# A hybrid attention encoder in fp32: the projections of z with v and of q with k as seven block products each

## The chip, the cores and the metric

The kernel runs on one core of one Trainium2 chip. TensorE (PE in the profile) multiplies, VectorE (DVE), ScalarE (ACT) and GpSimd (POOL) do the rest, and SyncE (SP) issues most of the DMAs. The metric is the device time of one launch in microseconds, lower is better. All tensors are float32.

## The reference, cut to what matters

Two layers. Each takes X (1024 tokens by 1024 channels), projects it to q, k, v (512 columns each), z (512) and x_c (256), mixes tokens in three ways, projects back, and then runs a SwiGLU block.

```python
h = rms_norm(x, norm_mix_g[l])
proj = h @ w_in[l]                       # 1024 x 2304
q, k, v, z_b, x_c = jnp.split(proj, splits, axis=-1)
mix_a = neighbourhood_attention(q, k, v, rpb)        # 8 heads
mix_b = spatial_gating(z_b, ...)         # gelu, layer norm of one half, 128x128 token matrix per head
mix_c = fourier_mix(x_c)                 # real part of a 2-D DFT over tokens and channels
mix = head_rms_norm(jnp.concatenate([mix_a, mix_b, mix_c], axis=-1), head_norm_g[l])
x = x + mix @ w_out[l]
h = rms_norm(x, norm_ffn_g[l])
x = x + (jax.nn.silu(h @ w_gate[l]) * (h @ w_up[l])) @ w_down[l]
```

## The kernel before, in words

**fp32 products out of three.** A float32 operand is split into a high part (rounded to the type fp32r, which TensorE reads at full rate) and the rest, the low part. `split3` (L1870 to L1874) issues three matmuls per tile into one PSUM bank: high by high, low by high and high by low. So each weight piece (128 by 1024, two k-tiles of 512 columns, 512 KB) is loaded by SP into a slot (`w_raw`), gets its high part on ACT (`piece_hi`, `w_hi`, L761) and its low part on POOL (`piece_lo`, `w_lo`, L675). POOL's instruction is what raises `w_ready`, for which PE waits before it uses a piece (`wait_piece`).

**Order of the work.** Nothing is scheduled at run time. Each engine has one list of instructions, written by hand, and they meet at semaphores. In a layer X lies transposed in SBUF, channels on the partitions: `x_res` raw, `h_hi` and `h_lo` times the norm's gain but not yet divided by the root mean square. PE makes x_c first (8 k-steps, 256 columns), then z, then a position DFT, then v, the spatial matrices and a channel DFT, then q, then k, then attention. A projection (`project`) fills all eight banks over eight k-tiles, 192 matmuls of 512 columns. The factor 1/rms is one number per token (`rstd_tok`, made on POOL by a power) and is put in when the banks are evicted: by ACT for z (with the gelu, L896), by ACT and DVE for v, by DVE for q and k (L1383, L1413, with the factor spread over the partitions by way of DRAM). Every result is a complete sum in its bank, evicted once. SP loads the pieces of the next projection while PE works on the last, and ACT's list has the `w_hi` of a projection's first pieces ahead of, or among, the evictions of the one before it.

**Around it.** DVE makes the Fourier butterflies (L1296 to L1309), the layer norm of z, the head norms of mix_b and mix_c (a reduction, a power of 32 columns on POOL at L695, a broadcast product at L1368), and in attention the logits (L1404). X stays in SBUF through attention and receives the out-projection and the SwiGLU result.

## Time and profile before

| | us |
|---|---|
| median of three runs | 2064.92 (2064.7 to 2065.62) |
| span of the profiled execution | 2062.8 |
| PE busy | 2042.2, 99% |
| DVE busy | 1419.9, 69% |
| ACT busy | 825.1, 40% |
| POOL busy | 227.8, 11% |

The span is from the first to the last instruction of one profiled execution; no time of its own is given for that execution beside it, and the runs lie 1.9 to 2.8 us above it. Start and length of an instruction in a timeline row are in microseconds from the span's start. TensorE's matmuls are pipelined, so a matmul of 0.39 us that starts 0.23 us after the one before it costs 0.23 us. An engine's busy share says little without the list it works through: what matters here is whether something that PE waits for is late. The profile has PE idle for 8.5 us at the start and for about 6 us in all after it.

### The profile page before, as it was taken

To read this page: it belongs to the slowest core of one execution; us is meant where nothing else is said; L and a number is where in the kernel's file an instruction comes from. 1 tells how busy PE (TensorE), PEld (TensorE's weight loads), DVE (VectorE), ACT (ScalarE), POOL (GpSimd) and SP (SyncE) were. 2 spreads that over 40 slices of the span, in tenths; PEclk is the share of its full clock that TensorE was granted. 3 is DMA by queue.
4 is the path that set the end of the run, shared out by engine and by line. 5 is a ranking of instruction groups with operands and counts; after the bars stand their busy time and mean duration, and the time that the engine had idled before them with its cause. 6 is when DMAs were issued, how large, how long until landed. Compare 5 with 4: busy or idle time off the path is not lost.

```text
span 2062.8 us, 27797 instructions
## 1 busy us (share of the span) xinstructions
PE 2042.2 (99%) x10316; PEld 1698.2 (82%) x10316; DVE 1419.9 (69%) x2320; ACT 825.1 (40%) x1466; POOL 227.8 (11%) x135
## 2 busy tenths in 40 slices
PE   8999999999999999999999999999999999999998
PEld 7888788888888888888898887888888888888887
DVE  6323773789877778787833338647988777778877
ACT  4221683452333333444612227634433333344443
POOL 1332034200000000000023301441000000000000
PEclk9999999999999999999999999999999999999999
DMA  5222443224333236633221314441243323383333
GB/s 183 72 92 62 144 134 123 72 77 169 130 111 107 98 112 255 195 97 97 76 86 62 102 41 144 144 153 48 85 172 129 114 93 111 109 310 114 97 98 123
DMA packets 111060, 244.40 MB, mean 118 GB/s; under 512 B 13648, under 2 KB 18640, under 8 KB 110672
## 3 DMA queue, kind: packets, MB, share of 16 engines
q1 hardware_dynamic: 97056, 214.32, 32.4%
q10 hardware_dynamic: 13872, 28.31, 3.7%
q8 instruction: 83, 1.36, 0.3%
q14 instruction: 49, 0.40, 0.1%
HBM read 191.73 MB, written 50.86 MB: 118 GB/s over the span
## 4 chain that ended last, share of the span: by engine, by line
PE 92%; DVE 5%; issue 1%; ACT 1%; DMA 0%; ACTq 0%; POOL 0%; DVEq 0%
PE bank L1872 28%; PE bank L1874 28%; PE bank L1873 28%; PE bank L2036 2%; PE bank L2055 2%; PE bank L2020 2%; DVE s_lo L1233 1%; DVE t_lo L1536 0%; PE bank L1966 0%; PE bank L2077 0%; PE bank L1995 0%; PE bank L2070 0%; ACT logits L950 0%; DVE hid_cu L1649 0%; ACT s_hi L797 0%
## 5 line engine op out<-in xcount | busy, mean ns | idle before, releaser
L1872 PE MATMUL bank<-t_hi,s_hi 128*128 128x512 f32 (+1 forms) x1336 | 516.9, 387 | 0.8 <-DVE hid_cu L1649 0.5
L1873 PE MATMUL bank<-t_lo,s_hi 128*128 128x512 f32 (+1 forms) x1336 | 516.3, 386 | 0.0
L1874 PE MATMUL bank<-t_hi,s_lo 128*128 128x512 f32 (+1 forms) x1336 | 516.3, 386 | 0.0
L1872 PEld LDWEIGHTS bank<-t_hi,s_hi 128*128 128x128 f32 x1336 | 250.9, 188 | 52.6 <-DVE hid_cu L1649 1.4
L1874 PEld LDWEIGHTS bank<-t_hi,s_lo 128*128 128x128 f32 x1336 | 250.9, 188 | 50.9
L1873 PEld LDWEIGHTS bank<-t_lo,s_hi 128*128 128x128 f32 x1336 | 250.9, 188 | 50.6
L675 POOL TENSOR_TENSOR w_lo<-w_raw,w_hi 128x1024 fp32r<-128x1024 f32 x65 | 161.1, 2492 | 928.9 <-ACT w_hi L761 787.4
L1872 PE MATMUL bank<-b_hi,s_hi 128*128 128x512 f32 x528 | 206.0, 390 | 0.2
L1874 PE MATMUL bank<-b_hi,s_lo 128*128 128x512 f32 x528 | 205.5, 389 | 0.0
L1873 PE MATMUL bank<-b_lo,s_hi 128*128 128x512 f32 x528 | 205.4, 389 | 0.0
L1872 PE MATMUL bank<-h_hi,w_hi 128*128 128x512 f32 x512 | 201.1, 393 | 0.0
L1874 PE MATMUL bank<-h_hi,w_lo 128*128 128x512 f32 x512 | 199.5, 390 | 0.0
L1873 PE MATMUL bank<-h_lo,w_hi 128*128 128x512 f32 x512 | 199.3, 389 | 0.0
L797 ACT ACTIVATE s_hi<-w_u 128x512 fp32r<-128x512 f32 x142 | 89.6, 631 | 233.0 <-PE bank L1874 176.3
L797 ACT ACTIVATE s_hi<-w_down 128x512 fp32r<-128x512 f32 x154 | 97.3, 632 | 200.7 <-PE bank L1874 199.9
L1233 DVE TENSOR_TENSOR s_lo<-w_down,s_hi 128x512 fp32r<-128x512 f32 x154 | 107.6, 699 | 75.8 <-ACT s_hi L797 75.7
L797 ACT ACTIVATE s_hi<-w_g 128x512 fp32r<-128x512 f32 x142 | 89.4, 630 | 163.9 <-PE bank L1874 104.9
L1872 PE MATMUL bank<-w_hi,h_hi 128*128 128x512 f32 (+1 forms) x384 | 137.4, 358 | 8.6 <-DVE h_lo L1128 8.5
L1873 PE MATMUL bank<-w_lo,h_hi 128*128 128x512 f32 (+1 forms) x384 | 136.6, 356 | 0.0
L1874 PE MATMUL bank<-w_hi,h_lo 128*128 128x512 f32 (+1 forms) x384 | 136.6, 356 | 0.0
L761 ACT ACTIVATE w_hi<-w_raw 128x1024 fp32r<-128x1024 f32 x67 | 70.3, 1058 | 127.5 <-DMA w_raw<-in_win 109.4
L1872 PEld LDWEIGHTS bank<-b_hi,s_hi 128*128 128x128 f32 x528 | 99.1, 188 | 21.3 <-issue 0.9
(218 smaller groups left out, 3187.2 us busy)
## 6 DMA issues: line engine op xcount, KB each, us to landing
w_g<-in_wg SPq DMA_DIRECT2D x44, 512.0 KB, 3.5
w_u<-in_wu SPq DMA_DIRECT2D x44, 512.0 KB, 4.4
t_raw<-hidden_t SPq DMA_DIRECT2D x88, 256.0 KB, 2.6
bias<-in_bias SPq DMA_DIRECT2D x24, 768.0 KB, 5.8
w_raw<-in_win SPq DMA_DIRECT2D x34, 512.0 KB, 3.8
t_raw<-hidden_b SPq DMA_DIRECT2D x66, 256.0 KB, 2.6
hidden_b<-hid_g SPq DMA_DIRECT2D x60, 256.0 KB, 2.0
hidden_t<-hid_x SPq DMA_DIRECT2D x44, 256.0 KB, 2.0
```

The lines of the kernel that those rows point to most:

```text
L675: nc.gpsimd.tensor_tensor(WL[s][:, :], WR[s][:, :], WH[s][:, :], ALU.subtract).then_inc(w_ready, 1)
L761: nc.scalar.activation(WH[s][:, :], WR[s][:, :], ACT.Copy).then_inc(w_hi, 1)
L797: nc.scalar.activation(SH[q % W_RING][:, :], weight_block(q), ACT.Copy).then_inc(s_hi, 1)
L1233: nc.vector.tensor_tensor(SL[q % W_RING][:, :], weight_block(q), SH[q % W_RING][:, :], ALU.subtract)\
L1872: nc.tensor.matmul(bank, lh, rh, start=start, stop=False)
L1873: nc.tensor.matmul(bank, lh, rl, start=False, stop=False)
L1874: return nc.tensor.matmul(bank, ll, rh, start=False, stop=stop)
L2020: mm = nc.tensor.matmul(score_bank(i, e).rearrange("p (r c) -> p r c", c=KC), qs[hp, c, q0:q0 + P], grid(ks[hp, c, :])[:, 4 * rr:4 * rr + ...
L2036: mm = nc.tensor.transpose(B[2 + t % 2][:, n * P:(n + 1) * P], L[:, t % 4, n * P:(n + 1) * P], IDENT[:, :])
L2055: mm = nc.tensor.matmul(B[VALUE_BANK][e * DH:(e + 1) * DH, c * P:(c + 1) * P], VB[j % 2][:, rr + n, h * DH:(h + 1) * DH], PT[:, h % 4, n * ...
```

## The change

q with k, and z with v, form two pairs. For each pair, X is cut into four blocks (token half by channel half: b11, b12, b21, b22), the two weight matrices into four (channel half by which of the two), and the two results, each in token halves, come out of seven block products instead of eight, in the Winograd form of Strassen's scheme. A block product is 16 tiles (4 banks by 4 k-tiles) of three matmuls. The 14 products are interleaved in the order of `IN_PRODUCTS`; the document numbers them n0 to n13 by their place in it. One group uses banks 4 to 7 (zv), the other banks 0 to 3 (qk). The banks are not cleared between most products: the sums run on in PSUM, and after each product its four banks are read out ("tapped") into a result, ACT writing and DVE adding.

Since blocks of different tokens are now added, X must be normalised before the products. 1/rms is turned and spread over the partitions by PE (`spread_tokens`), DVE multiplies X in place (`norm`, 16 instructions of 128x512), makes the block differences in place (`differences`, 16), and ACT and DVE split seven operands into high and low parts (`operand`, `operand_low`, 28 instructions each). Weight blocks are summed by POOL (`block_sum`, `third_sum`, 20 instructions of 128x1024 a layer), a sum that is used twice goes through DRAM (`w_sum_zv`, `w_sum_qk`), and 28 pieces a layer are split instead of 16. Raw X, now overwritten, is kept in DRAM (`x_scratch`; for layer 0 the input itself) and read back during attention.

```diff
+IN_PRODUCTS = (("zv", 2), ("qk", 2), ("qk", 1), ("zv", 1), ("zv", 6), ("qk", 6), ("qk", 7), ("zv", 7),
+               ("zv", 4), ("qk", 4), ("zv", 5), ("qk", 5), ("zv", 3), ("qk", 3))
+IN_TERMS = {2: ((1, 0),), 1: ((0, 0),), 6: ((0, 1), (0, 0), (1, 1)), 7: ((0, 1), (0, 0)), 4: ((1, 1),),
+            5: ((0, 1), (1, 1)), 3: ("s2", (1, 0))}
+ACT_TAPS = [n for n in range(NPROD) if IN_PRODUCTS[n][1] in (2, 6, 7) or IN_PRODUCTS[n] == ("qk", 4)]
...
 # GpSimd
+            def block_sum(l, n):
+
+                for i in range(2):
+                    s = ALL_SLOT[piece(n, i)]
+                    pool.wait_ge(w_landed[s], 16 * (l * PER_SLOT[s] + loads_before(piece(n, i)) + 2))
+                    nc.gpsimd.tensor_tensor(WR[s][:, :], WR[s][:, :], WT[s][:, :], ALU.add).then_inc(w_sum, 1)
+            def blocks_lo(l, *products):
+                for n in products:
+                    for i in range(2):
+                        if n in IN_THIRDS:
+                            pool.wait_ge(s2_stored, 16 * w_thirded(l, n, 1))
+                        piece_lo(l, piece(n, i))
...
+                blocks_lo(l, 4)
+                block_sum(l, 5)
+                third_sum(l, 5)
+                blocks_lo(l, 5)
+                pool.wait_ge(hs_var, l * 2 + 1)
+                nc.gpsimd.tensor_tensor(SR[:, :], SS[:, :], NHALF[:, :], ALU.pow).then_inc(hs_rstd, 1)
+                block_sum(l, 6)
+                blocks_lo(l, 6)
+                block_sum(l, 7)
+                blocks_lo(l, 7, 8, 9)
...
+                block_sum(l, 13)
                 pool.wait_ge(ln_var, l + 1)
                 nc.gpsimd.tensor_tensor(LR[:, :], LR[:, :], NHALF[:, 0:8], ALU.pow).then_inc(ln_rstd, 1)
...
 # ScalarE
+            def blocks_hi(l, *products):
+                for n in products:
+                    for i in range(2):
+                        piece_hi(l, piece(n, i))
+                def tap(n, *banks):
+
+                    g, product = IN_PRODUCTS[n]
+                    for j in banks or range(4):
+                        act.wait_ge(acc_full, full(l, n, j))
...
+                tap(4)
+                operand("t3")
+                blocks_hi(l, 5)
+                tap(5)
+                blocks_hi(l, 6)
+                tap(6)
+                operand("t4")
+                blocks_hi(l, 7)
+                tap(7)
+                operand("m1")
+                blocks_hi(l, 8)
+                tap(8)
+                blocks_hi(l, 9)
+                operand("b22")
+                tap(9)
+                blocks_hi(l, 10)
...
 # VectorE
+                def norm(k, h):
...
+                    nc.vector.scalar_tensor_tensor(out=X[:, k, half(h)], in0=X[:, k, half(h)], scalar=GM[:, k:k + 1],
+                                                   in1=(B[6] if h else RL)[:, :], op0=ALU.mult, op1=ALU.mult)\
+                        .then_inc(x_normed, 1)
+                for k in range(4):
+                    norm(4 + k, 1)
+                    if k:
+                        operand_low("b21", k - 1)
+                operand_low("b21", 3)
+                for k in range(4):
+                    norm(k, 1)
+                copy_xc(6, 7)
+                variance(0)
+                for k in range(4):
+                    operand_low("b11", k)
+                copy_xc(2, 3)
...
 # TensorE
+                    if j == 0 and k % 2 == 0:
+                        wait_piece(piece(n, k // 2))
...
+                for k in range(4):
+                    for j in range(2):
+                        in_ready(0, j, k)
+                        in_tile(0, j, k)
+                    if k == 1:
+                        sum_tokens(0)
+                spread_tokens(0)
+                in_bank(0, 2)
+                in_bank(0, 3)
+                in_product(1)
+                pe.wait_ge(fft_step, (l + 1) * FFT_STEPS)
...
+                position_dft(0, (4, 5, 6))
+                position_dft(1, (7, 4, 5))
+                in_bank(2, 0)
+                in_bank(2, 1)
...
+                pe.wait_ge(ab_act, l * 3 + 3)
+                pe.wait_ge(ab_dve, l * 3 + 3)
+                channel_dft(0)
+                channel_dft(1)
+                in_bank(2, 2)
+                in_bank(2, 3)
+                for n in range(3, NPROD - 1):
+                    in_product(n)
+                in_bank(NPROD - 1, 0)
+                pe.wait_ge(ln_step, l * 10 + 10)
+                spatial(0)
...
 # SyncE
+                for k in range(0, KT_D, 2):
+                    sp.dma_start(X[:, k:k + 2, :], (xscr if l else x)[k:k + 2].rearrange("k p n -> p k n"))\
+                      .then_inc(x_moved, 16)
```

**ScalarE in the middle of the projections.** Before, with `w_hi` the high parts of weight pieces (the number is the buffer) and `uv_tok` the evicted z:

```order
L761 ACTIVATE w_hi_80<-w_raw_104 128x1024 [waits w_landed2]
L761 ACTIVATE w_hi_78<-w_raw_102 128x1024 [waits w_landed0]
L761 ACTIVATE w_hi_79<-w_raw_103 128x1024 [waits w_landed1]
L896 ACT_TABLE_LOAD
L896 ACTIVATE uv_tok<-bank,rstd_tok 128x2x256 [waits acc_full] x8
```

The conversions wait for their landing alone and stand ahead of the evictions of z. In the changed kernel, from the taps of n4 (`v_tok`) over those of n5 (`q_raw`) to those of n6 (`k_raw`), where `w_hi_94` and `w_hi_95` are n5's weights, `104` and `105` those of n6, `96` and `97` those of n7:

```order
L1057 ACTIVATE v_tok<-bank 128x512 [waits acc_full] x4
L927 ACTIVATE in_t_hi<-x_res 128x512 [waits t_raw,acc_full] x4
L903 ACTIVATE w_hi_94<-w_raw_124 128x1024 [waits w_third]
L903 ACTIVATE w_hi_95<-w_raw_125 128x1024 [waits w_third]
L1060 ACTIVATE q_raw<-bank 128x8x4x16 [waits acc_full] x4
L903 ACTIVATE w_hi_104<-w_raw_134 128x1024 [waits w_sum]
L903 ACTIVATE w_hi_105<-w_raw_135 128x1024 [waits w_sum]
L1062 ACTIVATE k_raw<-bank 128x512 [waits acc_full] x4
L927 ACTIVATE in_t_hi<-x_res 128x512 [waits t_raw,acc_full] x4
L903 ACTIVATE w_hi_96<-w_raw_126 128x1024 [waits w_sum]
L903 ACTIVATE w_hi_97<-w_raw_127 128x1024 [waits w_sum]
```

The high parts of a product's weights now stand behind the four taps of the product before it.

**GpSimd in the same place.** Before, the low parts of v's and q's pieces around the layer norm's power:

```order
L675 TENSOR_TENSOR w_lo_90<-w_raw_102,w_hi_78 128x1024 [waits w_hi]
L690 TENSOR_TENSOR ln_rstd<-ln_rstd,minus_half 128x8 [waits ln_var]
L675 TENSOR_TENSOR w_lo_98<-w_raw_110,w_hi_86 128x1024 [waits w_hi]
L675 TENSOR_TENSOR w_lo_99<-w_raw_111,w_hi_87 128x1024 [waits w_hi]
L675 TENSOR_TENSOR w_lo_91<-w_raw_103,w_hi_79 128x1024 [waits w_hi]
```

In the changed kernel, from n4's low parts to n6's sums (L786 adds the second block, L793 the third):

```order
L774 TENSOR_TENSOR w_lo_111<-w_raw_126,w_hi_96 128x1024 [waits w_hi,s2_stored]
L774 TENSOR_TENSOR w_lo_112<-w_raw_127,w_hi_97 128x1024 [waits w_hi,s2_stored]
L786 TENSOR_TENSOR w_raw_124<-w_raw_124,w_term_139 128x1024 [waits w_landed0]
L786 TENSOR_TENSOR w_raw_125<-w_raw_125,w_term_140 128x1024 [waits w_landed1]
L793 TENSOR_TENSOR w_raw_124<-w_raw_124,w_term_139 128x1024 [waits w_landed0]
L793 TENSOR_TENSOR w_raw_125<-w_raw_125,w_term_140 128x1024 [waits w_landed1]
L774 TENSOR_TENSOR w_lo_109<-w_raw_124,w_hi_94 128x1024 [waits w_hi,s2_stored]
L774 TENSOR_TENSOR w_lo_110<-w_raw_125,w_hi_95 128x1024 [waits w_hi,s2_stored]
L820 TENSOR_TENSOR head_rstd<-head_ss,minus_half 128x32 [waits hs_var]
L786 TENSOR_TENSOR w_raw_134<-w_raw_134,w_term_149 128x1024 [waits w_landed10]
L786 TENSOR_TENSOR w_raw_135<-w_raw_135,w_term_150 128x1024 [waits w_landed11]
```

Between n4's low parts and n5's stand four sums, and n6's sums stand behind n5's low parts and a power.

**VectorE between the butterflies and the DFT's copies.** Before, from the last butterfly's successor to the copies of the DFT's banks (`dft_t`, which the channel DFT reads):

```order
L1309 SCALAR_TENSOR_TENSOR dft_69<-dft_sums,dft_even_odd 128x256 x4
L1317 BN_STATS bn_stats<-uv_tok 128x6 [waits z_ev]
L1320 BN_AGGR mean_var<-bn_stats 128x2 [waits ln_stat]
...
L1322 TENSOR_SCALAR ln_rstd<-mean_var 128x8 [waits ln_stat]
L1327 COPY dft_t<-bank 128x512 [waits dft_full] x2
L1327 COPY dft_t<-bank 128x256 [waits dft_full]
```

In the changed kernel, where `rstd_low` is 1/rms of the first token half, in SBUF, and `in_n` the operand of n4 and n5:

```order
L1579 SCALAR_TENSOR_TENSOR dft_86<-dft_sums,dft_even_odd 128x256 x4
L1487 SCALAR_TENSOR_TENSOR x_res<-x_res,g_mix,rstd_low 128x512 [waits x_squared,xc_act] x8
L1503 TENSOR_TENSOR x_res<-x_res 128x512 [waits x_normed]
L1506 SCALAR_TENSOR_TENSOR in_n_85<-x_res 128x512 [waits t_raw,acc_full]
L1509 SCALAR_TENSOR_TENSOR x_res<-in_n_85,x_res 128x512 [waits t_raw]
L1511 SCALAR_TENSOR_TENSOR x_res<-in_n_85,x_res 128x512
L1592 COPY dft_t_70<-bank 128x512 [waits dft_full] x2
L1592 COPY dft_t_70<-bank 128x256 [waits dft_full]
```

Eight normalisations and four differences, all from SBUF to SBUF, have moved ahead of the copies.

## Rows read from the trace of the kernel before

**Rows 1.** The page: span, and the engines' busy time
```profile
span 2062.8 us, 27797 instructions
PE 2042.2 (99%) x10316; PEld 1698.2 (82%) x10316; DVE 1419.9 (69%) x2320; ACT 825.1 (40%) x1466; POOL 227.8 (11%) x135
```

**Rows 2.** Timeline, TensorE: start, length, engine, line; four places
```profile
35.05 0.47 PE L1872 MATMUL bank<-w_hi,h_hi 128*128 128x512 f32 x1
...
73.65 0.39 PE L1872 MATMUL bank<-w_hi,h_hi 128*128 128x512 f32 x1
...
78.41 0.39 PE L1872 MATMUL bank<-w_hi,h_hi 128*128 128x512 f32 x1
...
223.26 0.45 PE L2020 MATMUL bank<-k_hi,q_hi 64*128 64x384 f32 x2
...
369.56 1.05 PE L1866 MATMUL bank<-ident,rstd_tok_ffn 128*128 128x128 f32 x8
```

**Rows 3.** Busy time of each engine in the stretch of z, v, q and k
```profile
core 0: us, PE busy (x) PEld busy (x) DVE busy (x) ACT busy (x) POOL busy (x), PEclk, DMA share, GB/s
35.00:223.30 188.30, 188.20 (x846) 155.00 (x845) 67.49 (x91) 43.59 (x61) 48.01 (x18) 1.00 0.21 65
```

**Rows 4.** Timeline, TensorE at the start
```profile
8.87 0.41 PE L1873 MATMUL bank<-w_lo,h_hi 128*128 128x256 f32 x1
...
12.47 0.28 PE L1872 MATMUL bank<-w_hi,h_hi 128*128 128x256 f32 x1
12.59 0.28 PE L1873 MATMUL bank<-w_lo,h_hi 128*128 128x256 f32 x1
```

**Rows 5.** Groups of instructions by line: busy us, mean ns, idle before
```profile
L675 POOL TENSOR_TENSOR w_lo<-w_raw,w_hi 128x1024 fp32r<-128x1024 f32 x65 | 161.1, 2492 | 928.9 <-ACT w_hi L761 787.4 <-DVE t_lo L1243 111.6 <-DVE w_lo L1249 29.7
L761 ACT ACTIVATE w_hi<-w_raw 128x1024 fp32r<-128x1024 f32 x67 | 70.3, 1058 | 127.5 <-DMA w_raw<-in_win 109.4 <-DMA w_raw<-in_wom 16.0 <-DMA w_raw<-in_wout 2.1
L695 POOL TENSOR_TENSOR head_rstd<-head_ss,minus_half 128x32 f32<-128x32 f32 x4 | 21.7, 5429 | 12.4 <-DVE head_ss L1363 12.4
L959 ACT ACTIVATE k_hi<-k_raw 128x512 fp32r<-128x512 f32 x16 | 10.1, 632 | 63.2 <-DVE k_raw L1413 63.2
L1391 DVE TENSOR_TENSOR k_lo<-k_raw,k_hi 128x512 fp32r<-128x512 f32 x16 | 11.1, 693 | 11.2 <-ACT k_hi L959 11.2
L1413 DVE SCALAR_TENSOR_TENSOR k_raw<-bank,rstd_mix 128x512 f32<-128x512 f32 x16 | 11.1, 692 | 53.1 <-PE bank L1874 53.1
L680 POOL TENSOR_TENSOR rstd_tok_ffn<-rstd_tok_ffn,minus_half 128x4 f32<-128x4 f32 x5 | 5.0, 1006 | 648.8 <-DVE rstd_tok_ffn L1152 614.6 <-DVE rstd_tok_ffn L1523 34.2
```

**Rows 6.** Timeline, VectorE, Fourier sums of layer 0
```profile
38.98 1.23 DVE L1296 TENSOR_TENSOR dft_even_odd<-xc_tok 128x1024 f32<-128x1024 f32 x1
40.12 3.42 DVE L1297 TENSOR_TENSOR dft_even_odd<-xc_tok 128x1024 f32<-128x1024 f32 x1
...
46.33 1.43 DVE L1309 SCALAR_TENSOR_TENSOR dft<-dft_sums,dft_even_odd 128x256 f32<-128x256 f32 x4
```

**Rows 7.** Timeline of layer 1: VectorE, then GpSimd
```profile
1060.30 2.77 DVE L1299 TENSOR_TENSOR dft_sums<-dft_even_odd 128x512 f32<-128x512 f32 x1
...
1056.38 6.14 POOL L675 TENSOR_TENSOR w_lo<-w_raw,w_hi 128x1024 fp32r<-128x1024 f32 x2 [2.68 <-ACT w_hi L761]
```

**Rows 8.** Timeline, VectorE and GpSimd in the attention's tail
```profile
312.20 0.68 DVE L1455 COPY att_heads<-bank 128x512 f32<-128x512 f32 x1
...
311.52 4.75 POOL L675 TENSOR_TENSOR w_lo<-w_raw,w_hi 128x1024 fp32r<-128x1024 f32 x2
```

**Rows 9.** DMA issues: count, KB each, us to landing
```profile
w_raw<-in_win SPq DMA_DIRECT2D x34, 512.0 KB, 3.8
```

**Rows 10.** Timeline, VectorE, first scores of layer 0
```profile
224.29 0.56 DVE L1404 CUSTOM_DVE_ANT_0 logits<-bank,bias 128x384 f32<-128x384 f32 x1 [0.20 <-PE bank L2020]
227.67 0.55 DVE L1404 CUSTOM_DVE_ANT_0 logits<-bank,bias 128x384 f32<-128x384 f32 x1
```

**Rows 11.** Busy time and DMA in a stretch of attention
```profile
255.00:270.00 15.00, 15.00 (x163) 12.42 (x161) 11.75 (x35) 13.17 (x37) 4.53 (x5) 1.00 0.04 9
```

More of the change, by code:

```diff
@@ L80, with loads_before @@
+LOADS = [1, 1] + [len(IN_TERMS[product]) for _, product in IN_PRODUCTS for _ in range(2)] + [1] * 16
+SLOTS = 15
+USED_ORDER = list(range(OUT_P, OUT_P + 7))
+PER_SLOT = [sum(n for t, n in zip(ALL_SLOT, LOADS) if s == t) for s in range(SLOTS)]
+def loads_before(p):
+    return sum(n for t, n in zip(ALL_SLOT[:p], LOADS) if t == ALL_SLOT[p])
 BANKS = [4, 5, 6, 7, 0, 1, 2, 3]
@@ L84 @@
 FFT_STEPS = 13
[L86 to L88 removed]
+X_ORDER = [(k, 1) for k in range(KT_D)] + [(k, 0) for k in range(KT_D)]
 PRODUCTS = (1, 2, 5, 6, 3, 7, 4)
@@ L123, in x_final, with summed @@
     return (20, 28)[k >= 4] + k % 4 + 1 if h else (36, 40)[k >= 4] + k % 4 + 1
-def summed(order, i):
-    h = order[i][1]
-    second = [j for j, (_, hh) in enumerate(order) if hh == h][1]
-    last = max(i, second)
-    return sum(order[j] != next(o for o in order if o[1] == order[j][1]) for j in range(last + 1))
+def summed(i):
+    return i - (i > 8)
 KB = 1024
@@ new lines, in load_block, with load_blocks, store_sum @@
+            def load_block(l, n, t):
+                for i in range(2):
+                    load_piece_of(l, n, t, i)
+            def load_blocks(l, n, behind=None):
+                if behind is not None:
+                    sp.wait_ge(acc_full, full(l, behind, 3))
+                for t in range(min(len(IN_TERMS[IN_PRODUCTS[n][1]]), 2)):
+                    load_block(l, n, t)
+            def store_sum(l, n):
+                for i in range(2):
+                    sp.wait_ge(w_third, w_thirded(l, n, i))
+                    sp.dma_start(sscr[IN_PRODUCTS[n][0]][i], WR[ALL_SLOT[piece(n, i)]][:, :]).then_inc(s2_stored, 16)
@@ L457, in load_out, with store_values @@
+            def store_values(n, first):
+                for j in range(4):
+                    b = first + j
+                    wait_tapped(sp, l, n, j)
+                    sp.dma_start(vscr[b * P:(b + 1) * P, :], VN[:, b, :]).then_inc(v_stored, 16)
             def load_out(l, p):
@@ new lines, in operand @@
+                def operand(name):
+                    for k in range(4):
+                        in_operand_hi(l, name, k)
+                blocks_hi(l, 0)
+                for i in range(12, 16):
+                    x_hi(l, *X_ORDER[i])
+                    x_square(l, i)
+                operand("b21")
+                copy_xc(4, 5)
+                blocks_hi(l, 1)
+                operand("b11")
+                copy_xc(0, 1)
+                act.wait_ge(r_spread, 2 * l + 2)
+                nc.scalar.activation(RL[:, :], B[1][:, :], ACT.Copy).then_inc(xc_act, 1)
@@ new lines, in _ @@
+                operand("t3")
[13 more added lines that the diff above has]
+                blocks_hi(l, 10)
+                act.wait_ge(acc_full, full(l, 9, 3))
+                for c in range(4):
+                    act.wait_ge(tap_act, l * 4 * len(ACT_TAPS) + 4 * ACT_TAPS.index(9) + c + 1)
+                    nc.scalar.activation(KH_[:, c, half(1)], KR_[:, c, half(1)], ACT.Copy).then_inc(qk_hi, 1)
@@ new lines, in _ @@
+                differences(0)
+                for b in range(3):
+                    dve.wait_ge(dft_full, l * 8 + 3 + b + 1)
+                    a = slice(2 * b, min(2 * b + 2, 5))
+                    nc.vector.tensor_copy(AB[1][:, a, :],
+                                          B[(7, 4, 5)[b]][:, 0:256 * (a.stop - a.start)]
+                                          .rearrange("p (a n) -> p a n", n=256)).then_inc(ab_dve, 1)
+                for k in range(1, 4):
+                    tap(2, k - 1)
+                    differences(k)
+                    operand_low("n2", k - 1)
@@ L1471, in _ @@
                     else:
-                        key_rest(7)
+                        for c in range(4):
+                            query_rest(0, c)
                     if i == 5:
@@ L1960, in position_dft, with in_bank, in_product @@
+                def in_bank(n, j):
+                    for k in range(4):
+                        in_ready(n, j, k)
+                        if n == NPROD - 1 and j == 3 and k == 2:
+                            scores(0)
+                        in_tile(n, j, k)
+                def in_product(n):
+                    for j in range(4):
+                        in_bank(n, j)
                 def position_dft(f, banks):
```

908 lines of the change are left out of this document (517 added, 391 removed).

## The prediction, made before the changed kernel ran

> **What bounds the kernel now.** I read the page first: PE busy 2042 of 2063 us [rows 1]. Only PE's time counts, and any wait of PE beyond today's handful is a loss. The timeline of PE then gives its price: 21 matmuls of 128x512 from 73.65 to 78.41, 0.2267 us each [rows 2]. In layer 0 z starts at 35.05 and the first scores stand at 223.26 [rows 2]; in this stretch PE is busy for 188.20 of 188.30 us, with DVE at 67, ACT at 44, POOL at 48 us and the DMA at 0.21 [rows 3]. So the projections run at PE's full rate, and the others only have to be on time. The question is therefore what each engine's list makes PE wait for afterwards, and I went through the five lists for that, with durations from the groups by line [rows 5].
>
> **What it removes.** A layer has 768 matmuls of 512 columns for z, v, q and k; 14 products of 48 are 672. 96 x 0.2267 = 21.8 us a layer saved, 43.5 in all. One product is 10.9 us. This is certain, since it is a count of PE work.
>
> **What it adds on PE.** Two spreads a layer, of four transposes (eight instructions) each, 0.8 us apiece (369.56 to the next matmul at 370.37 [rows 2]): 1.6.
>
> **What it adds on POOL.** 28 low parts and 20 sums in place of 16 low parts. A low part costs 2.4 (two take 4.75 [rows 8]; the mean of 2.49 holds some stretched ones [rows 5]). The trace has no POOL sum of f32; it has the same two inputs and size as a subtraction, so 2.4; from below it could be no less than half (two powers of 32 columns take 5.4 each and 4 columns 1.0 [rows 5], so its price is not by bytes alone), from above 3.1 (two low parts stretched to 6.14 beside DVE [rows 7]). 48 x 2.4 = 115 us a layer, within the 188 of the stretch, but in bursts.
>
> **DVE beside POOL.** On DVE an addition from SBUF to SBUF starts at 40.12 and takes 3.42, while its twin takes 1.23 [rows 6]; another takes 2.77 where a low part runs on POOL [rows 7]. A copy from PSUM beside POOL keeps its 0.68 [rows 8]. I conclude that a two-input operation within SBUF waits until the running POOL operation ends. In the new list 16 norms, 16 differences and 28 operand low parts are of this kind. Alone one is 0.69 (`k_lo` [rows 5]); in a string against back-to-back POOL operations each costs a whole one, 2.4 + 0.6 = 3.0. Bounds: 0.69 (nothing blocks) and 3.42 [rows 6].
>
> **The chain between products.** This is what decides. PE finishes bank 3 of product n; ACT taps it (0.63, as `k_hi` of that size [rows 5]), and only then, by its list, makes the high part of n+1's first piece (1.06), POOL its low part (2.4), and only then may PE start n+1. With 0.2 of drain and 0.2 of semaphores that is 4.5 us of idle PE before n6, n9 and n10. Before n5, n7 and n8 ACT also has four operand conversions, 4 x 0.63 = 2.5, in the way: 7.0. In the old list the conversions stand ahead of the evictions, which is why PE never waits there [rows 3]. The second piece's low part comes 2.4 after the first, which feeds only 6 matmuls, 1.36: + 1.04 each time. Special cases: before n5 POOL has two sums, two thirds whose third term is loaded after the second (512 KB in 3.8 [rows 9]), and a store: 7.5 instead of 7.0; before n6 it has the power of 32 columns (5.4 [rows 5]) and two sums, and DVE's head scaling beside it: 5.3. Together 8.5 + 6.4 + 8.0 + 8.0 + 5.5 + 5.5 = 41.9 us a layer. n11 and n12 have their weights in time, since ACT makes them apart from the last taps.
>
> **Ahead of n5.** The first spread waits for the power of 4 columns (1.0 [rows 5]) behind two low parts on POOL: 3.0 in layer 0, 0 in layer 1, where they are made earlier. The other spread waits until DVE has done norms, x_c copies, variance and four low parts, some blocked: 6.5 (7.2 in layer 1). Then DVE does its butterflies, 6.6 us without the blocked piece (38.98 to 47.76, less 2.2 [rows 6]), and eight norms and four differences opposite eight POOL operations that run back to back, before it copies the DFT's banks: PE waits 2.4 before the position DFT and 2.8 before the channel DFT, 5.2 in all.
>
> **The end.** The layer norm's power now stands on POOL behind the sums of n13, and n13's low parts behind that. PE waits 4.0 for its first piece, 3.3 for the second, and 4.2 before the spatial matrices for the two passes over 2048 columns, `q_lo` and `k_lo` that stand between on DVE: 11.5. In attention the third logits come 3.4 after the first today (224.29 and 227.67 [rows 10]); afterwards between them stand the power (5.4), head scaling of 2048 columns (2 x 1.14, the pitch of 1024 in [rows 6]) and four `q_lo` (2.6), with 1.0 for the scaling before the power: 11.3, so + 7.9.
>
> **Hidden.** X's return is 4 MB, in a stretch where DMA is at 0.04 [rows 11] and nothing needs it before the out-projection: nothing; uncovered it would be some 30 us (8 x 3.8 [rows 9]). The stores and further loads: DMA at 0.21 [rows 3], nothing; if one is late, see the rivals. 16 taps on DVE from PSUM replace evictions of the same kind (0.69, L1413 [rows 5]).
>
> **PE's clock after a wait.** From 8.87 to 12.47, after PE's first idle 8.5 us, 17 matmuls of 256 columns start at a pitch of 0.21; from 12.47 to 12.59 it is 0.12 [rows 4]. That is the lower level (1.2 GHz) and then the upper (2.4). A restart after a long wait thus costs 17 x (0.21 − 0.12) ≈ 1.6 to 1.8 us. The trace has such a restart only after 8.5 us of idling, none after 2 to 5 us. I charge it to the waits of 6.5 and more and to nothing shorter: the one before the second spread (1.8) and those before n5, n7 and n8, where the slow matmuls fall partly into the wait for the second piece (0.8 each): 4.2 a layer, 8.4 in all. Bounds: 0 and a charge for each wait, 13.8 a layer.
>
> The Trainium skill ("TensorE: Matmul & The Clock Gate", section "Part 1: The HAM clock gate") says that an array that idles falls back to 1.2 GHz and that sustained work gives 2.4 back; it sets no charge per wait that I could take over. The trace agrees at its one place, the first 3.6 us of work at half pitch [rows 4]. If each of the new waits counted as such, my sum would go to the upper bound, which is the first rival.
>
> **The sum.** Layer 0: 3.0 + 1.6 + 6.5 + 5.2 + 41.9 + 11.5 + 7.9 = 77.6, less 21.8 = + 55.8. Layer 1: 0 + 1.6 + 7.2 + 5.2 + 41.9 + 11.5 + 7.9 = 75.3, less 21.8 = + 53.5. With 8.4 for the clock, + 117.7. On the profiled execution 2062.8 [rows 1] becomes 2180.5; the median lies 2.1 above its span and becomes 2064.9 + 117.7 = 2182.6.
>
> **Rivals.**
> Every wait, the short ones too, restarts PE at the lower level: 13.8 a layer in place of 4.2. For it, the start [rows 4]; against it, no short wait in the trace shows it either way. 2064.9 + 109.3 + 27.6 = 2202.
>
> DVE and POOL hardly hinder each other in a string, and only the chain between products stays (40.5, some of n5's and n6's extra gone), with 5.2 at the DFTs, 1.6, 5 at the end and 6 in attention: 58.3 − 21.8 = 36.5 a layer, 2138. For it, only two of the traced DVE operations that I name are blocked; against it, the butterfly that is blocked to 3.42 [rows 6].
>
> Loads come late: a block's second and third terms take another 4 to 5 us each beside one another (8.3 instead of 3.8), about 9 a layer at n5 and the sums after it: 2200. Against it, DMA at 0.21 [rows 3].
>
> The other side: PE never waits between products, because ACT and POOL convert n+1's weights while PE works on n. The saving then stands, less the spreads: 2064.9 − 43.5 + 3.2 = 2024.6. It decides from the point where `w_hi` of n+1 is made before the last tap of n. The old list does it [rows 3], and there are over 6 us of ACT and POOL time free per product; the new list puts the taps first for six products of fourteen, so it can't hold for those. Even if all else were free, 6 x 4.5 a layer of chain is 54, more than the 43.5 saved. That the change isn't what it says is not to be seen: the count is 672.
>
> **How the numbers follow.** The forecast has 0.72, the clock at every wait 0.13, little hindrance 0.10, late loads 0.03, the other side 0.02. The unknown prices: the POOL sum at 3.1 instead of 2.4 adds some 10 us over 20 sums a layer of which a third are in PE's way; the strings on DVE at 0.69 take off up to 20; the clock's bounds are −8 and +19. So the forecast alone goes from 2150 to 2212, and the range with parts of its rivals from 2125 to 2222. Less than 0.2% can't be told from no change; faster by more 0.02, within 0.01, slower 0.97.
>
> **What would show it.** PE's list of idle times: before n5, n7, n8 about 7 to 8.5 us, before n6, n9, n10 about 4.5 to 5.5, each ended by POOL's low part, and one of about 1 us six matmuls later; none before n11 and n12. First scores of layer 0 at about 271 (275 with the clock) instead of 223.3. POOL busy for about 115 us of each projection stage. Norms on DVE at about 3 us beside POOL. Matmuls at a pitch of 0.4 for some 3 us behind the longest waits only. Wrong it would be if the waits between products are ended by something else or are missing, or if the pitch of whole products is off 0.2267.

## The result, and the profile after

The changed kernel takes 2196.49 us (2195.94 to 2199.15), the kernel before 2065.14: slower by 6.4% (ratio 1.0638, 95% interval 1.0623 to 1.0654). 2182 was forecast, in a range of 2125 to 2222. Of 131 us lost 118 were foreseen. Of all the runs below one was slow (one of four of dft_act, 7211 us at a granted clock of 0.39), and its ratio is made without it.

The page of the changed kernel, first lines (beside [rows 1]):

```profile
span 2194.1 us, 28110 instructions
## 1 busy us (share of the span) xinstructions
PE 2053.7 (94%) x10156; PEld 1694.8 (77%) x10156; DVE 1548.5 (71%) x2463; ACT 903.6 (41%) x1611; POOL 405.8 (18%) x202
```

The span grew by 131.3. PE has 160 instructions fewer (192 matmuls less, 32 of the spreads more) and is yet busy for longer, 2053.7 against 2042.2. So the loss has two forms: PE idles, and PE is busy at a slower clock. The waits of PE over the whole run (engine, line, who released it: us, times, longest):

```profile
PE bank L2158 <- POOL w_lo L774: 75.2, 17, 8.7
PE bank L2309 <- DVE minus_max L1693: 15.9, 2, 8.0
PE bank L2272 <- ACT dft_t L1090: 10.9, 2, 5.7
PE bank L2191 <- DVE xc_tok L1475: 10.7, 2, 5.8
PE bank L2158 <- DVE h_lo L1331: 9.6, 1, 9.6
PE bank L2288 <- DVE v_tok L1527: 7.6, 2, 3.8
```

Of these only the wait for `h_lo`, at the start, was there before. 75 us are waits for the low part of a weight piece, made by POOL. What such a wait is made of is seen between n6 and n7 of layer 0, in the timeline (start, length, engine, line; the bracket is the idle time before and who ended it):

```profile
162.47 0.39 PE L2160 MATMUL bank<-in_t_hi,w_lo 128*128 128x512 f32 x1
162.90 0.60 ACT L1062 ACTIVATE k_raw<-bank 128x512 f32<-128x512 f32 x1 [2.12 <-PE bank L2160]
163.39 2.18 ACT L927 ACTIVATE in_t_hi<-x_res 128x512 fp32r<-128x512 f32 x4
165.47 1.99 ACT L903 ACTIVATE w_hi<-w_raw 128x1024 fp32r<-128x1024 f32 x2
166.59 4.67 POOL L774 TENSOR_TENSOR w_lo<-w_raw,w_hi 128x1024 fp32r<-128x1024 f32 x2 [10.33 <-ACT w_hi L903]
168.99 0.79 PE L2158 MATMUL bank<-w_hi,in_t_hi 128*128 128x512 f32 x1 [6.12 <-POOL w_lo L774]
```

The tap, four operand conversions, the high part, the low part: each step begins only when the one before it is done or nearly so, since ACT's list has them in this order. POOL had idled for 10.33 us before. The matmuls that follow, and two from far behind a wait:

```profile
169.58 0.63 PE L2159 MATMUL bank<-w_lo,in_t_hi 128*128 128x512 f32 x1
170.00 0.63 PE L2160 MATMUL bank<-w_hi,x_lo 128*128 128x512 f32 x1
...
233.56 0.39 PE L2159 MATMUL bank<-w_lo,in_m_hi 128*128 128x512 f32 x1
233.79 0.39 PE L2160 MATMUL bank<-w_hi,x_lo 128*128 128x512 f32 x1
```

Other starts of layer 0 that waited for POOL, before n5, n6, n9, and both pieces of n13:

```profile
131.20 0.80 PE L2158 MATMUL bank<-in_n_hi,w_hi 128*128 128x512 f32 x1 [8.54 <-POOL w_lo L774]
149.30 0.80 PE L2158 MATMUL bank<-in_t_hi,w_hi 128*128 128x512 f32 x1 [4.05 <-POOL w_lo L774]
205.66 0.80 PE L2158 MATMUL bank<-in_t_hi,w_hi 128*128 128x512 f32 x1 [4.06 <-POOL w_lo L774]
260.24 0.80 PE L2158 MATMUL bank<-in_b_hi,w_hi 128*128 128x512 f32 x1 [2.95 <-POOL w_lo L774]
264.60 0.50 PE L2158 MATMUL bank<-in_b_hi,w_hi 128*128 128x512 f32 x1 [1.43 <-POOL w_lo L774]
```

From 169.58 the matmuls start 0.43 apart; at 233.56, far from a wait, 0.23, as before [rows 2]. That is 1.2 and 2.4 GHz; the granted clock is 0.50 from 169.6 to 174.0 and 1.00 from 233.5 to 236.0. Layer 0 from 35 to 300 us had 90 starts at the slow pitch, which cost 20.1 us, layer 1 has 74, 17.1 us (pitch less 0.2267, summed over the rows). A few of these starts are of the spatial product, whose pitch is 0.43 at the full clock too, and two of its matmuls at the lower clock, 0.85 apart, are left out; with both put right the cost is 20.8 and 17.2.

The first scores of layer 0 stand at 282.2, those of layer 1 at 1364.3 (before: 223.26 [rows 2] and 1242.2). With 8.0 us more of waiting just behind them, layer 0 lost 66.9 us and layer 1 63.2, 130.1 of the 131.3.

### The profile page after: what moved, and what is told of

Its sections match the earlier page's. It is cut to its first block, busy times and chain, and to the rows that moved or that the text cites. A ratio compares the mean times of both kernels' runs of the same rounds, so it can differ in the third digit from the quotient of the medians.

```text
span 2194.1 us, 28110 instructions
## 1 busy us (share of the span) xinstructions
PE 2053.7 (94%) x10156; PEld 1694.8 (77%) x10156; DVE 1548.5 (71%) x2463; ACT 903.6 (41%) x1611; POOL 405.8 (18%) x202
## 4 chain that ended last, share of the span: by engine, by line
PE 80%; DVE 7%; POOL 6%; issue 3%; ACT 3%; DMA 1%; ACTq 0%; DVEq 0%; SPq 0%; POOLq 0%
PE bank L2158 24%; PE bank L2159 24%; PE bank L2160 24%; POOL w_lo L774 4%; PE bank L2360 2%; PE bank L2379 2%; POOL w_raw L786 2%; PE bank L2309 2%; ACT w_hi L903 1%; DMA w_raw<-in_win 1%; DVE q_lo L1645 1%; DVE s_lo L1433 1%; POOL head_rstd L836 0%; DVE x_sq_sum_first L1346 0%; PE bank L2288 0%
## 5 line engine op out<-in xcount | busy, mean ns | idle before, releaser
L774 POOL TENSOR_TENSOR w_lo<-w_raw,w_hi 128x1024 fp32r<-128x1024 f32 x90 | 234.7, 2626 | 927.8 <-ACT w_hi L903 804.3
L779 POOL TENSOR_TENSOR rstd_tok_ffn<-rstd_tok_ffn,minus_half 128x4 f32<-128x4 f32 x5 | 5.0, 1006 | 648.6 <-DVE rstd_tok_ffn L1352 614.5
L903 ACT ACTIVATE w_hi<-w_raw 128x1024 fp32r<-128x1024 f32 x91 | 93.0, 1050 | 63.2 <-DMA w_raw<-in_win 30.5
L2160 PEld LDWEIGHTS bank<-b_hi,s_lo 128*128 128x128 f32 x528 | 99.1, 188 | 20.7
L2159 PEld LDWEIGHTS bank<-b_lo,s_hi 128*128 128x128 f32 x528 | 99.1, 188 | 20.3
L1443 DVE TENSOR_TENSOR t_lo<-t_raw,t_hi 128x512 fp32r<-128x512 f32 x154 | 105.5, 685 | 8.7 <-ACT t_hi L969 8.7
L1433 DVE TENSOR_TENSOR s_lo<-w_g,s_hi 128x512 fp32r<-128x512 f32 x142 | 97.4, 686 | 10.7 <-ACT s_hi L963 10.7
L2158 PE MATMUL bank<-h_hi,w_hi 128*128 128x512 f32 x256 | 101.1, 395 | 0.0
```

The source lines that it names most:

```text
L774: nc.gpsimd.tensor_tensor(WL[s][:, :], WR[s][:, :], WH[s][:, :], ALU.subtract).then_inc(w_ready, 1)
L903: nc.scalar.activation(WH[s][:, :], WR[s][:, :], ACT.Copy).then_inc(w_hi, 1)
L1433: nc.vector.tensor_tensor(SL[q % W_RING][:, :], weight_block(q), SH[q % W_RING][:, :], ALU.subtract)\
L1443: nc.vector.tensor_tensor(TL[t][:, :], TR[t][:, :], TH[t][:, :], ALU.subtract).then_inc(t_lo, 1)
L2158: nc.tensor.matmul(bank, lh, rh, start=start, stop=False, skip_group_check=reopened)
L2159: nc.tensor.matmul(bank, lh, rl, start=False, stop=False, skip_group_check=reopened)
```

## The experiments

Times are medians; "changed kernel" is 2196.49 us, and all ratios are to the kernel before, which ran beside each of them at 2065.05 to 2065.86.

**hi_first: the conversions of n+1 inside the taps of n.** For n = 4 to 9, on ScalarE:

```diff
-                tap(6)
-                operand("t4")
-                blocks_hi(l, 7)
+                tap(6, 0)
+                blocks_hi(l, 7)
+                tap(6, 1, 2, 3)
+                operand("t4")
```

> ScalarE converts the two weight pieces of n+1 behind the first tap of n instead of behind the fourth (n = 4 to 9). Theory (the order of ScalarE's list makes the waits between the products): the waits before n7 to n10 (6.3, 6.3, 4.2, 4.2 us a layer) go, and with them some 7.7 us of matmuls at half pitch; n6 keeps about 3 of 4.2 (power and sums on GpSimd stand before it) and n5 its 8.7 (the store of its sum). 30 us a layer: 2196.5 - 60 = about 2137 us. Rival (GpSimd has too much to do, and the order only shows it): the waits come back in front of n7 to n10 as waits for GpSimd, and half or less is gained, 2165 or more.

2144.25 us, ratio 1.0380 (1.0365 to 1.0396): 52 gained of 60 expected. Its waits of PE:

```profile
PE bank L2164 <- POOL w_lo L774: 40.5, 12, 10.1
PE bank L2315 <- DVE minus_max L1699: 15.9, 2, 8.0
PE bank L2278 <- ACT dft_t L1090: 10.9, 2, 6.2
```

The waits before n7 to n10 are gone in both layers; n6 keeps 3.2 and 4.3, n5 8.7 and 10.3. The 8 us that are missing of the 60 stand at n13, whose wait grew from 3.1 to 5.0, in n5 of layer 1, in n6, and in the slow pitch, which fell by 12 us where 15 were expected. The order of one list made the waits before n7 to n10, and POOL had room for the same work earlier.

**small_sums: GpSimd's sums cut, the order kept.** Both sums of weight blocks:

```diff
-nc.gpsimd.tensor_tensor(WR[s][:, :], WR[s][:, :], WT[s][:, :], ALU.add)
+nc.gpsimd.tensor_tensor(WR[s][:, 0:8], WR[s][:, 0:8], WT[s][:, 0:8], ALU.add)
```

> The 20 sums of weight blocks a layer add 8 columns instead of 1024 (the rest of each sum is left out), so GpSimd has some 50 us a layer less to do, with every wait and the order as it was. Theory (order, not load): the waits before n6 to n10 stay, n5 loses 2 to 3 us and n13 some, stretched VectorE operations shorten: about 2185 us. Rival (GpSimd's load and its contention with VectorE make the loss): 2150 us or less.

2177.08 us, ratio 1.0538 (1.0521 to 1.0556): 19 gained. The waits before n6 to n10 are 4.2, 6.3, 6.3, 4.2, 4.2 us with the sums and without them. So the load of POOL isn't their cause. The 19 come from n5 (8.7 to 6.4), the DFT (5.4 to 3.0) and n13.

**fill: PE kept busy in the waits.** TensorE, ahead of the weights' waits of n5 to n10:

```diff
+FILL = {5: 34, 6: 16, 7: 25, 8: 25, 9: 16, 10: 16}
...
+                        for i in range(FILL[n]):
+                            nc.tensor.matmul(B[bank][:, :], t[:, 0, 0:P], t[:, i % 4, :], start=False,
+                                             stop=i == FILL[n] - 1, skip_group_check=True)
```

> TensorE does 16 to 34 matmuls of 512 columns with operands it has while it would wait for the weights of n5 to n10 (they add to a bank, so the result is changed). Theory (the lower clock after each of these waits comes from the idling): the matmuls at half pitch behind n5 to n10 go (13.2 us a layer), the wait for the second piece comes back to 1.04 six times, so 7 us a layer less, about 2182 us. Rival (the half pitch has another cause, such as late weights): 2196 us with the same half pitch. If only waits over 6.5 us had the charge, as my forecast assumed, the gain would be 2 to 3 us a layer.

2187.39 us, ratio 1.0591 (1.0575 to 1.0606): 9 gained where 14 were expected. The mechanism is plain all the same. Windows over n5 to n12 of layer 0, first of the changed kernel, then of this one (us; busy time of PE, PEld, DVE, ACT, POOL; PEclk, DMA share, GB/s):

```profile
122.00:256.00 134.00, 101.04 (x382) 79.76 (x382) 45.51 (x55) 46.09 (x70) 78.93 (x31) 0.86 0.33 119
```

```profile
122.00:252.00 130.00, 120.92 (x519) 96.22 (x518) 45.46 (x54) 45.91 (x69) 80.04 (x31) 1.00 0.35 126
```

The granted clock goes from 0.86 to 1.00; of 58 starts at the slow pitch (13.0 us) none is left. Nothing but filler was added, so idling caused them, after the waits of 4.1 us too. The weights are no earlier, so what PE gains in clock it partly waits for again: with fast matmuls the second piece is late by 0.8 us at n5 to n8 and by 1.3 at n9 and n10, which matmuls at the lower clock had hidden.

**dft_act and dft_dve: what holds the position DFT.** In the changed kernel PE waits 5.2 us there. The timeline of SyncE's queue, ScalarE and PE:

```profile
69.84 3.14 SPq L527 DMA_DIRECT2D w_term<-in_win  x2
...
70.65 1.05 ACT L903 ACTIVATE w_hi<-w_raw 128x1024 fp32r<-128x1024 f32 x1
...
73.02 2.05 SPq L527 DMA_DIRECT2D w_raw<-in_win  x3
...
78.48 1.06 ACT L903 ACTIVATE w_hi<-w_raw 128x1024 fp32r<-128x1024 f32 x1 [6.79 <-DMA w_raw<-in_win]
79.45 1.34 ACT L1090 ACTIVATE dft_t<-bank 128x512 f32<-128x512 f32 x3
...
80.08 1.22 PE L2272 MATMUL bank<-twiddle,dft 128*128 128x256 f32 x2 [5.21 <-ACT dft_t L1090]
```

ScalarE waits for n3's second piece, which SyncE issues only behind n4's third terms (69.84; its own issue is among those at 73.02), and the DFT's copies stand behind it. dft_act moves that one conversion behind the copies:

```diff
-                blocks_hi(l, 3)
+                piece_hi(l, piece(3, 0))
...
                         .then_inc(ab_act, 1)
+                piece_hi(l, piece(3, 1))
```

> The changed kernel with one edit: ScalarE converts the second weight piece of n3 behind its copies of the DFT's banks, not ahead of them. Theory (the wait of 5.4 and 5.8 us before the second position DFT comes from a load that SyncE issues late and behind which ScalarE's copies stand): this wait falls to about 1, with some half pitch, 2196.5 - 8 to 12 = 2184 to 2188 us. Rival (my forecast's cause, VectorE's norms and differences stretched beside GpSimd's sums): no change, 2196.

dft_dve moves what my forecast had named:

```diff
-                differences(0)
                 for b in range(3):
...
                                           .rearrange("p (a n) -> p a n", n=256)).then_inc(ab_dve, 1)
+                differences(0)
```

> The changed kernel with one edit: the first four differences on VectorE stand behind its copies of the DFT's banks. My forecast's cause (these stretched operations hold the copies) gives 5 us or more, under 2190. The theory from the trace (a late load holds ScalarE) gives nothing: 2196.

dft_act: 2182.87 us, ratio 1.0569 (1.0554 to 1.0585), 13.6 gained, and the wait is gone in both layers. dft_dve: 2194.06 us, ratio 1.0628 (1.0614 to 1.0642), 2.4 gained, which the intervals don't tell from nothing. The late load held PE. VectorE's differences had a small part in it all the same, by another way than the forecast's: in dft_dve the wait falls from 5.4 and 5.8 us to 3.5 and 4.5, and the DFT begins 1.5 us sooner behind the second spread in both layers. SyncE may load the third terms only when GpSimd's first sums of n4 are made, and beside the differences these take longer. The two sums in the changed kernel, then in dft_dve:

```profile
66.97 5.62 POOL L786 TENSOR_TENSOR w_raw<-w_raw,w_term 128x1024 f32<-128x1024 f32 x2
...
67.04 4.73 POOL L786 TENSOR_TENSOR w_raw<-w_raw,w_term 128x1024 f32<-128x1024 f32 x2
```

This is also why small_sums shortened the wait to 3.0.

**att: the head scaling later.** VectorE:

```diff
                 tap(13, 3)
-                head_scale(1, MB)
...
+                    if i == 2:
+                        head_scale(1, MB)
```

> The changed kernel with one edit: mix_b's head scaling on VectorE, which waits for GpSimd's power of 5.4 us, stands behind the sixth logits of the layer instead of ahead of the third. Forecast's step (the power and the scaling cost 7.7 of the 8.0 us wait in attention, four low parts the rest): the wait of 8.0 falls to about 2.8, 2196.5 - 2 x 5.2 = about 2186 us. Rival (the wait is moved, since the tiles of mix_b are turned soon after): 2192 or more.

2187.87 us, ratio 1.0592: 8.6 gained of 10.4. The wait at the second scores falls from 8.0 to 2.8 in both layers.

**all_moved: all of it at once.** hi_first, dft_act, and on GpSimd each power ahead of the pieces it stood behind (the head norm's behind n6's), n5's sums ahead of n4's low parts, n13's high parts earlier on ScalarE, head scaling after six logits:

```diff
-                blocks_lo(l, 4)
                 block_sum(l, 5)
                 third_sum(l, 5)
+                blocks_lo(l, 4)
...
-                block_sum(l, 13)
                 pool.wait_ge(ln_var, l + 1)
                 nc.gpsimd.tensor_tensor(LR[:, :], LR[:, :], NHALF[:, 0:8], ALU.pow).then_inc(ln_rstd, 1)
+                block_sum(l, 13)
```

> The same work in another order: ScalarE converts n+1's pieces behind the first tap of n, n13's ahead of k's last high parts, and n3's second piece behind the DFT copies; GpSimd makes n5's sums ahead of n4's low parts, each power of rstd, head and layer norm ahead of (or, for the head norm, behind) the weights it stood beside; VectorE scales mix_b's heads after six logits. Theory (the loss is all order): waits fall from 63 to under 10 us a layer and the half pitch with them, 2064.9 - 43.5 + 3.2 + 10 to 20 = 2035 to 2045 us, faster than the kernel before. Rival (the pipeline's own latencies of landing, sum, high and low part don't fit between two products): 2065 to 2090.

2105.04 us, ratio 1.0191 (1.0176 to 1.0206). 91 of 131 us are back, but neither theory is right: no product waits long for its pipeline (n7 2.8 us, n12 0.8), and still 30 us of waits a layer remain. Its waits:

```profile
PE bank L2296 <- DVE v_tok L1534: 22.0, 2, 11.0
PE bank L2280 <- ACT dft_t L1090: 14.0, 2, 7.2
...
PE bank L2166 <- POOL w_lo L774: 7.5, 6, 2.6
PE bank L2199 <- DVE xc_tok L1482: 6.1, 2, 3.5
```

The two large ones end in VectorE. Its timeline in all_moved, and in the middle what GpSimd does then:

```profile
67.00 11.64 DVE L1494 SCALAR_TENSOR_TENSOR x_res<-x_res,g_mix,rstd_low 128x512 f32<-128x512 f32 x8
...
69.91 5.54 POOL L793 TENSOR_TENSOR w_raw<-w_raw,w_term 128x1024 f32<-128x1024 f32 x2
...
78.68 1.36 ACT L1090 ACTIVATE dft_t<-bank 128x512 f32<-128x512 f32 x3 [11.25 <-DVE x_res L1494]
...
182.78 11.09 DVE L1646 TENSOR_TENSOR k_lo<-k_raw,k_hi 128x512 fp32r<-128x512 f32 x4
206.41 11.00 DVE L1662 TENSOR_SCALAR uv_tok<-uv_tok,mean_var,ln_rstd 128x256 f32<-128x256 f32 x8 [6.15 <-POOL ln_rstd L832]
```

In the changed kernel the same eight norms took 5.38 us with POOL idle beside them. Here four `k_lo` take 11.09 beside back-to-back sums and low parts, 2.8 each for 0.69 of work [rows 5]. Once the order no longer leaves POOL idle, VectorE is what it pushes aside.

**dft_pool: GpSimd holds back.** all_moved, and:

```diff
                 blocks_lo(l, 2)
+                pool.wait_ge(x_normed, l * 16 + 16)
                 block_sum(l, 4)
```

with n3's second piece loaded ahead of n4's third terms.

> The kernel all_moved, and GpSimd starts the sums of n4 only when VectorE has normalised X's second half; SyncE loads n3's second piece ahead of n4's third terms. Theory (an operation of GpSimd keeps VectorE's two-input operations within SBUF out, so that less GpSimd work at that time makes TensorE faster): the wait of 7.3 and 7.0 us at the second position DFT falls under 2 and its half pitch with it, 2105 - 12 to 15 = 2090 to 2093 us. Rival (GpSimd's sums are then late and n4 or n5 waits instead): 2100 or more.

2101.83 us, ratio 1.0177 (1.0162 to 1.0191): 3 us less than all_moved, which is the rival's case. The wait of 7.3 at the DFT is gone, and one of 6.1 stands before n4, ended by VectorE's `v_tok`. What was won at one place was paid at the next.

**all2, all3, all4: VectorE's strings cleared.** all2 brings the layer norm's power and its passes earlier (n12's sum ahead of n10's low parts), spreads k's low parts between taps, and makes and uses the first rstd sooner. all3 moves copies, one tap and the head norm's reduction. all4 takes eight differences off n4's path, for which the operand has memory of its own:

```diff
-        N2 = at("in_n2", IN_LO_AT["n2"], [P, 4, HALF])
+        N2 = at("in_n2", IN_LO_AT["b21"], [P, 4, HALF])
...
                 operand_low("n2", 3)
+                tap(3, 1, 2)
+                for k in range(4):
+                    differences_rest(k)
```

> dft_pool, and: the sum of n12 ahead of n10's low parts, the layer norm's power ahead of n12's low parts and its passes with less GpSimd work beside them, k's low parts between the taps of n10 or behind the last taps, the head power behind n7's low parts, the rstd of the first half made and used earlier, q's last low parts between the first logits. Theory: of the waits left in all_moved (11.2 at the spatial matrices, 2.8 at n7, 3.7 at the spread, 2.8 in attention) most go, with their half pitch: 2090 - 2 x 18 = about 2055 us, faster than the kernel before by about 0.5%. Rival (GpSimd has 126 us of work a layer in 190 and VectorE can't be kept clear of it): the waits only move, 2075 to 2090.

> all2, and six moves more: VectorE copies the DFT's banks ahead of the first four differences; ScalarE makes n4's high parts before the last two of the operand n2; the first tap of n3 stands before the last differences; the head norm of mix_b is reduced behind the first two logits and scaled after the sixth; v's rows are loaded ahead of the second bias tile. Theory: of 15 us of waits a layer left in all2 (2.3 at the channel DFT, 5.1 at n4, 2.2 and 3.0 and 2.1 in attention) 8 to 10 go, with 2 of half pitch: 2072.4 - 20 to 24 = 2048 to 2052 us, faster than the kernel before by 0.6 to 0.8%. Rival (the waits only move to what is next on VectorE): 2062 or more.

> all3, and in VectorE's list the eight differences that only n6 and n8 need (t3, t4) stand behind n4's operand, which is kept in memory of its own; the last query tap stands ahead of the head norm's reduction; v's values are stored ahead of the first bias tile. all3 waits 11.1 us a layer at n4 because 20 two-input operations of VectorE run beside GpSimd's eight there, some 2.7 us each. With 12 of them on the path they end some 11 us earlier. Theory: the wait falls to 0 to 2, with 1 to 2 of half pitch and 2 in attention gained: 2066.2 - 20 to 28 = 2038 to 2046 us, faster than the kernel before by 1 to 1.3%. Rival (the eight moved differences push n5 or n6 back in turn): 2055 or more.

all2: 2072.38 us, ratio 1.0042 (1.0029 to 1.0055). all3: 2066.24 us, 1.0004 (0.9996 to 1.0013), no difference from the kernel before. all4: 2056.60 us, ratio 0.9959 (0.9945 to 0.9973), faster than both kernels, by 8.5 and 139.9 us. All three missed their figure, and most of what was missing stood at n4, where a VectorE string meets POOL: all2 had counted on 2090 for dft_pool and still waited 5.1 us there, in all3 this wait grew to 11.1 as others went, and in all4 it fell by half. The waits of all3, then those of all4:

```profile
PE bank L2181 <- DVE q_raw L1549: 21.9, 2, 11.0
...
PE bank L2402 <- issue: 5.1, 2, 2.6
```

```profile
PE bank L2189 <- DVE q_raw L1554: 10.0, 2, 5.1
PE bank L2340 <- DVE minus_max L1722: 4.9, 4, 1.3
PE bank L2410 <- issue: 4.1, 2, 2.1
```

The moved differences are those of t3 and t4, for n6 and n8. The wait at n4 fell from 11.0 to 5.1 a layer, not to nothing: of the 12 operations that stayed, nine still took 2.0 to 2.9 us in layer 0, beside POOL.

**all3_small: what the sums still cost.** all3 with the small sums.

> all3 with the 20 sums of weight blocks a layer cut to 8 columns (the rest of each sum is left out). It prices what GpSimd's sums still cost through VectorE in a good order. If contention is what is left: under all3 by 4 to 10 us. If the order hides it: within 2 us of all3.

2041.30 us, ratio 0.9884 (0.9869 to 0.9899): 24.9 under all3, far more than the 4 to 10 expected. The stretch of n2 and n3 of layer 0, in all3 and in all3_small:

```profile
66.00:106.40 40.40, 29.51 (x151) 24.98 (x151) 37.70 (x28) 10.72 (x19) 31.99 (x12) 0.92 0.61 208
```

```profile
66.00:104.00 38.00, 37.48 (x186) 31.68 (x186) 28.29 (x35) 13.70 (x23) 15.74 (x14) 1.00 0.70 249
```

With half of POOL's time gone, DVE does 35 instructions in 28 us instead of 28 in 38, and PE no longer waits. PE's wait at n4 is 0.7 and 1.1 us there, in all3 it is 11.1. The rest to what the saving promises, 2065.2 − 43.5 + 3.2 for the spreads = 2025, is 16 us.

## Why the forecast was right, and where it was off

Its ledger against the traces, us a layer (layer 0 / layer 1 where they differ; a measured wait is the distance of two starts less 0.2267, so 4.2 is what the brackets show as 4.05):

| step | forecast | measured |
|---|---|---|
| 96 matmuls less | −21.8 | −21.8 (pitch 0.2267 again) |
| two spreads on PE | 1.6 | 1.6 (not measured apart) |
| first spread | 3.0 / 0 | 0.5 / 0 |
| second spread | 6.5 / 7.2 | 6.0 / 5.0 |
| DFTs | 5.2 | 5.4 / 5.8, other cause |
| n5 to n10 | 41.9 | 33.9 / 34.7 |
| n13, spatial (1.0 of it a gap behind the spatial matmuls) | 11.5 | 9.9 |
| attention | 7.9 | 8.0 |
| slow clock | 4.2 | 20.1 / 17.1 |
| waits under 1 us and the rest | 0 | 3.3 / 2.9 |
| sum | 60.0 / 57.7 | 66.9 / 63.2 |

**The chain between products** was right in kind and place. hi_first shows it by taking it away, small_sums by leaving it alone. 7.0 and 4.5 were forecast for n7, n8 and n9, n10; 6.3 and 4.2 came. Four conversions in a row take 2.18, not 4 x 0.63, as they overlap. Before n6 the power and the sums of POOL were over in time (5.3 forecast, 4.2 measured). Before n5 the wait was 8.7 for 7.5, where the low part waits for the store of its sum. I had named this store but priced it with the sums at 0.5 us in all; POOL idled 5.8 us for it:

```profile
128.80 4.66 POOL L774 TENSOR_TENSOR w_lo<-w_raw,w_hi 128x1024 fp32r<-128x1024 f32 x2 [5.81 <-DMA w_sum_qk<-w_raw]
```

No run takes this wait away alone.

**The step that failed is the clock.** I charged the lower level to waits of 6.5 us and more, "and to nothing shorter", 4.2 us a layer. The changed kernel's timeline shows the slow pitch after waits of 2.95 and 4.05 us as after 8.5. fill shows that idling is its cause. 37.2 us in place of 8.4: this term was too small by 29 us, more than the 14 by which the whole forecast missed. That the total came so near is partly luck: the waits of all steps together were forecast 23 us too long, which hides most of it. The argument for the charge was weak from the start: "none after 2 to 5 us" was read from a trace in which, after the first 8.5 us, no wait of PE is longer than 1.6 us, so that it could show nothing on waits between. The rival with this mechanism, 2202, was nearer to 2196 than my own number, though I gave it 0.13.

I had read the page of the Trainium skill as giving no charge for a wait. That was a misreading. "TensorE: Matmul & The Clock Gate", section "HAM oscillation — how this bites in real kernels", describes a kernel in which short bursts of matmuls alternate with waits of 3 to 5 us for data and each burst begins cold. The traces agree: 11, 7 and 7 slow starts behind the three waits of 4.2 us in layer 0.

**Two terms were not additive.** I added 1.04 us six times for the second piece, and slow matmuls on top. At the slow pitch six matmuls take 2.6 us, and the second low part comes 2.35 after the first: in the changed kernel the wait for it is nearly gone, and in fill it is back (0.8 and 1.3 us). This is 6 of the 8 us a layer by which n5 to n10 came out under the forecast.

**The DFT's term was right in size by chance.** Stretched operations opposite eight of POOL were to hold it. The norms ran while POOL was nearly all the time idle (5.38 for eight). The four differences did take 2.8 each, but VectorE's own copy was not what PE waited for: a load queued late behind a wait of SyncE held ScalarE (dft_act), and the differences added 1.5 us of the 5.4 and 5.8 to it through GpSimd's sums (dft_dve). In all_moved, where that load is out of the way, my mechanism appears, with 7.2 us.

**The price of VectorE beside POOL**, 3.0 us an operation from [rows 6, 7], was right where POOL's instructions stand back to back: 2.7 to 2.9. Where POOL pauses it is less: the eight norms of all_moved took 11.64, 1.5 each, since POOL idled for the last 3 us of them. POOL's own load was forecast at 115 us a layer and measured at 134.5 from 35 to 300 us of layer 0. The rival in which this hardly matters (2138) is refuted by all3_small against all3. The rival in which PE never waits (2025) is the bound; all4 stops 32 us short of it. Loads did land later, 5.8 and 6.8 us for pieces and terms in the median against 3.8 [rows 9], but POOL waited for them only 1.5 us in layer 0.

The 16 us a layer that all4 leaves against the bound are 10.0 and 9.7 of waits over 1 us and some slow pitch: the granted clock was at half for 6.8 us of layer 0 and 10.2 of layer 1, which costs at most half of that, 3.4 and 5.1. The rest, some 2 us, is not assigned. Sums on another engine, or made ahead of the layer, were not tried.

## What to carry to other kernels

An algorithm that saves matmuls is paid for in the pipeline that feeds them: count, for each product, what its operands still have to pass through after the last event they are queued behind, in the lists of all engines. A wait of TensorE costs its own length and then, here, a restart at half clock, about 2 us each behind the waits of 3 us and more, so many short waits are dearer than their sum. And before work is given to an idle GpSimd, look at what VectorE does then: in these traces each operation of a string of two-input SBUF operations beside a busy GpSimd cost a whole GpSimd instruction.
